# Three more groups of gate and up as seven block products, and the down weights' corner loads in two parts

## The reference

```
def swiglu(x, w_gate, w_up, w_down):          # 1024 x 2816, 1024 x 2816, 2816 x 1024
    return (jax.nn.silu(x @ w_gate) * (x @ w_up)) @ w_down

def half_ffn(h, l, j):
    y = swiglu(rms_norm(h, ffn_norm_pre[l, j]), ffn_w_gate[l, j], ffn_w_up[l, j], ffn_w_down[l, j])
    return h + 0.5 * rms_norm(y, ffn_norm_post[l, j])

for l in range(2):
    h = half_ffn(h, l, 0)
    h = h + rms_norm(mixer_l(rms_norm(h, ...)), ...)
    h = h + rms_norm(cross_attention(rms_norm(h, ...), mem, ...), ...)
    h = half_ffn(h, l, 1)
```

## Time and profile before

| | us |
|---|---|
| three timed executions | 2294.86, 2297.34, 2299.69 |
| their median | 2297.34 |
| the profiled execution's own time | 2292.94 |
| its span, first to last instruction | 2291.0 |
| PE busy | 2263.8 |
| DVE busy | 1483.9 |
| ACT busy | 1049.7 |
| mean granted clock of PE | 0.998 |

### The profile page before, as it was taken

The page is one execution under the profiler, slowest core; times in us unless marked ns, Lnnn a source line. Parts: engine busy times, 40 slices in busy tenths (PEclk is TensorE's granted clock), DMA queues, the critical chain, the costliest instruction groups (busy, mean ns, idle before and its releaser), DMA issues. The chain is left out here.

```text
span 2291.0 us, 32607 instructions
## 1 busy us (share of the span) xinstructions
PE 2263.8 (99%) x12963; PEld 1969.5 (86%) x12963; DVE 1483.9 (65%) x1913; ACT 1049.7 (46%) x1627; POOL 102.8 (4%) x145
## 2 busy tenths in 40 slices
PE   8999999999999999999999999999999999999998
PEld 7888888888888888889988889988878888888997
DVE  5757445586545658577757567746896565756774
ACT  5433324544544444435544435535265554343652
POOL 0000003100000000000010000000000000000000
PEclk9999999999999999999999999999999999999999
DMA  4342332321222233415534315542322222431563
GB/s 170 104 136 74 98 106 73 111 67 62 74 75 99 64 127 134 142 52 139 165 129 166 124 42 147 166 157 92 101 75 83 93 65 95 154 125 56 133 175 110
DMA packets 181757, 249.84 MB, mean 109 GB/s; under 512 B 13832, under 2 KB 125800, under 8 KB 181608
## 3 DMA queue, kind: packets, MB, share of 16 engines
q1 hardware_dynamic: 177176, 232.00, 31.2%
q0 software_dynamic: 4320, 15.73, 3.5%
q10 hardware_dynamic: 112, 0.03, 0.0%
HBM read 222.54 MB, written 9.44 MB: 101 GB/s over the span
## 5 line engine op out<-in xcount | busy, mean ns | idle before, releaser
L2477 PE MATMUL ps<-xlo,whi 128*128 128x512 f32 (+1 forms) x1936 | 670.9, 347 | 6.2 <-issue 4.1
L2479 PE MATMUL ps<-xhi,whi 128*128 128x512 f32 (+1 forms) x1936 | 668.1, 345 | 0.0
L2478 PE MATMUL ps<-xhi,wlo 128*128 128x512 f32 (+1 forms) x1696 | 600.4, 354 | 0.0
L1533 DVE TENSOR_TENSOR wlo<-raw,whi 128x1024 fp32r<-128x1024 f32 x251 | 306.3, 1223 | 323.0 <-ACT whi L917 320.6
L917 ACT ACTIVATE whi<-raw 128x1024 fp32r<-128x1024 f32 x281 | 294.9, 1054 | 340.8 <-PE ps L2479 298.4
L2477 PEld LDWEIGHTS ps<-xlo,whi 128*128 128x128 f32 x1936 | 367.4, 190 | 51.7 <-issue 7.5
L2479 PEld LDWEIGHTS ps<-xhi,whi 128*128 128x128 f32 x1936 | 367.3, 190 | 44.2
L2478 PEld LDWEIGHTS ps<-xhi,wlo 128*128 128x128 f32 x1696 | 321.4, 189 | 43.4
L1539 DVE SCALAR_TENSOR_TENSOR wlo<-raw,vec,whi 128x512 fp32r<-128x512 f32 (+1 forms) x224 | 154.8, 736 | 154.1 <-ACT whi L921 153.5
L921 ACT ACTIVATE whi<-raw,vec 128x512 fp32r<-128x512 f32 (+1 forms) x224 | 145.4, 702 | 197.9 <-PE ps L2479 163.2
L2477 PE MATMUL ps<-wlo,xhi 128*128 128x512 f32 x352 | 138.6, 394 | 1.1 <-issue 1.1
(11 more groups left out here) (322 smaller groups left out, 3829.4 us busy)
## 6 DMA issues: line engine op xcount, KB each, us to landing
raw<-ffn_w_gate_dram SPq DMA_DIRECT2D x176, 256.0 KB, 3.0
raw<-ffn_w_up_dram SPq DMA_DIRECT2D x176, 256.0 KB, 3.2
raw<-ffn_w_down_dram SPq DMA_DIRECT2D x96, 256.0 KB, 3.0
w<-ffn_w_down_dram SPq DMA_DIRECT2D x72, 256.0 KB, 5.4
raw<-xattn_w_kv_dram SPq DMA_DIRECT2D x64, 256.0 KB, 3.0
lo_aside<-raw POOLq DMA_DIRECT2D x30, 512.0 KB, 5.5
raw<-even_w_in_dram SPq DMA_DIRECT2D x56, 256.0 KB, 2.8
raw<-odd_w_in_dram SPq DMA_DIRECT2D x42, 256.0 KB, 2.9
```

The costliest lines, as they stand in the source:

```text
L1533: v.tensor_tensor(flat(wlo[:, slot]), flat(raw[:, from_slot]), flat(whi[:, slot]).bitcast(f32), SUB).then_inc(lo_made, 1)
L2477: mm(out_ap, lh, rl, start=start, stop=False, skip_group_check=skip_group_check)
L2478: mm(out_ap, ll, rh, start=False, stop=False, skip_group_check=skip_group_check)
L2479: return mm(out_ap, lh, rh, start=False, stop=stop, skip_group_check=skip_group_check)
```

## The change

`WOVEN` now holds groups 3, 4 and 5 too, so in the last three SwiGLUs the middle gate-and-up stage also runs as three woven groups: nine groups in all. `weave` on DVE takes the pass of the `quads` behind it and places the four corner combinations inside the stage's last group. The corner loads of that stage are issued in two parts, five behind group 3's weight loads and four behind group 4's, each part behind a wait of SP for the group's accumulation into the low part of B21.

```diff
-WOVEN = (6, 7, 8, 9, 10)
+WOVEN = (3, 4, 5, 6, 7, 8, 9, 10)
+ORDER_OF_CORNERS = [(corner, q) for corner in range(3) for q in range(QUADS)]
...
-                        if piece and after in pass_of and g == (2 if n == 0 else 1) and kp < 3:
-                            load_corners(pass_of[after], l, j, (kp,))
+                        if piece and after in pass_of and not scaled_rows(kind, l, arg) and g == (2 if n == 0 else 1) and kp < 3:
+                            load_corners(pass_of[after], l, j, [(kp, q) for q in range(QUADS)])
+                        if after in pass_of and scaled_rows(kind, l, arg):
+                            if n == 0 and g == 2 and kp < 3:
+                                load_corners(pass_of[after], l, j, [(kp, q) for q in range(QUADS)])
+                            if n == 1 and g < 2 and kp == 3:
+                                sp.wait_ge(raw_added[1], 16 * (woven_group[n_stage, g] + 1))
+                                first = ORDER_OF_CORNERS[:5] if g == 0 else ORDER_OF_CORNERS[5:]
+                                load_corners(pass_of[after], l, j, first)
...
-        def weave(w, group, mids, held_mid):
+        def weave(w, group, mids, held_mid, next_pass):
...
                     block_low(g, held)
+            if next_pass is not None:
+                t1_sums(next_pass)
             split_next()
...
             v.tensor_tensor(c11[:], y_out, c11[:], ADD).then_inc(c11_ready, 1)
             split_next()
+            if next_pass is not None:
+                t2_sums(next_pass, 0, late)
             dve.wait_ge(product_kept, 3 * w + 2)
             unit_done("T3")
             v.tensor_tensor(c22[:], x_out, c22[:], ADD).then_inc(c22_ready, 1)
             split_next()
+            if next_pass is not None:
+                t3_sums(next_pass, 0, late)
...
             split_next()
+            if next_pass is not None:
+                t4_sums(next_pass, 0, late)
             dve.wait_ge(gate_silu, mids).then_inc(bank_free[bank // 4], 1)
...
+                        if g == ng - 1 and not plain:
+                            split_next()
```

More of the change, by code:

```diff
@@ L618, in load, with load_corners @@
                 sp.dma_start(dst, src).then_inc(raw_full[slot], 16)
-        def load_corners(k, l, j, corners=range(3)):
+        def load_corners(k, l, j, corners=ORDER_OF_CORNERS):
             base, _, q0 = passes[k]
@@ L629, in load_corners @@
                     sp.wait_ge(pieces_used, base - 4 * FF_GROUPS[0][1] + 1 + SPLIT_SLOTS)
-            for n in corners:
+            for n, q in corners:
                 t, loaded, odd, c0 = ((w11, w11_loaded, 1, 0), (w12, w12_loaded, 1, GC), (w21, w21_loaded, 0, 0))[n]
-                for q in range(QUADS):
-                    k0 = (2 * (q0 + q) + odd) * P
-                    sp.dma_start(t[:, q, :], w[k0:k0 + P, c0:c0 + GC]).then_inc(loaded, 16)
+                k0 = (2 * (q0 + q) + odd) * P
+                sp.dma_start(t[:, q, :], w[k0:k0 + P, c0:c0 + GC]).then_inc(loaded, 16)
         def last_corner(w, k0, n):
@@ L2081, in _ @@
                         mids += 1
-                        weave(woven_group[n_stage, g], E.group, mids, held_mid)
+                        weave(woven_group[n_stage, g], E.group, mids, held_mid, pass_of.get(after) if g == ng - 1 else None)
                     for kp in range(0 if woven(kind, l, arg, g) else 4):
```

## The result

| | before | after |
|---|---|---|
| median of five timed executions, us | 2297.34 | 2304.82 |
| lowest and highest | 2294.84 to 2299.69 | 2303.43 to 2309.32 |
| ratio after to before, 95% interval | | 1.0034 [1.0023, 1.0045] |
| span of the profiled execution | 2291.0 | 2301.7 |

The prediction was 2294.7 us, with a range of 2286.5 to 2304.0: it missed by 10.1 us, and the sign was wrong.

What follows compares the result with a forecast made beforehand. PE bounds the kernel, with a DVE, ACT and DMA chain level with it in woven groups. Per stage 3.16 - 0.3 - 0.8 - 1.2 = 0.86 us gained, 2.6 in three stages: 2294.7 us, range 2286.5 to 2304.

Steps and rivals of the forecast that it cites:

- cover: In `quads` DVE is busy 26.1 of 28.7 us; the 2.6 us left was counted as enough for the combinations behind c22.
- (e): T4 of group 5 waits for DVE's add into c22, 3.1 us late, less 1.9 for PE's late start: 1.2 us.
- (a): Middle stage: seven products for eight take each group from 21.76 to 20.16 us, a ceiling of 4.80 us per stage.
- (b): Waits woven groups bring to the middle stage, taken from the last stage's first three groups: 1.64 us per stage.
- (d): DVE's block work (2.65 us) in groups 4 and 5 delays group 5's accumulation: 0 to 2.35 us, taken as 0.8.
- (c): Corner loads: SP's wait for group 3's B21 accumulation delays group 4's weights; 0 to 3.8 us per stage, taken as 0.3.
- The clock: The granted clock is at 1.00 of its 2.4 GHz level in every window read, so it was given no effect.
- the chain through DVE, ACT and the accumulation: Rival: this chain becomes the bound in the middle stage, 3.1 us lost per stage, 2306.6 us, slower; chance 0.15.
- the marks that I named for being wrong: Signs against: groups 4 and 5 start over 2 us late each, T4 of group 5 waits 3 us, or `quads` lengthens.

Runs made afterwards that it cites:

- e11: The changed kernel with only group 3 of the middle stage woven and the corner loads where the kernel before has them: 2293.40 us, ratio 0.9981.
- e5: The changed kernel with DVE's four block sums and first subtraction cut to one column where a woven group follows: 2296.57 us, ratio 0.9996.
- e3: The changed kernel with DVE's add into c22 moved ahead of the next split, T1 sum and second combination in every woven group: 2308.72 us, ratio 1.0050.
- e1: The changed kernel with each corner load of the middle stages moving one row of 128, SP's wait kept: 2303.03 us, ratio 1.0022.
- e6: The changed kernel with DVE's four corner combinations inside group 5 cut to one column: 2297.81 us, ratio 1.0003.
- e9: The changed kernel with DVE's two block subtractions moved behind the add into c22 in groups 4 and 5: 2308.02 us, ratio 1.0049.
- e4: The changed kernel with group 5 of the middle stage computed plainly again, corner loads unchanged: 2294.50 us, ratio 0.9990.
- e7: As e4, but no corner loads behind group 3: six behind group 4, three in group 5: 2291.81 us, ratio 0.9975.
- e8: The changed kernel run once more, unaltered, for its spread: 2306.33 us, ratio 1.0038.

## Why the prediction was wrong

**The step that failed.** Per stage the sum set 3.94 us of waits against a ceiling of 4.80 and kept 0.86. Measured in the first profile were 5.98 us of waits, and middle stage and `quads` together got 1.58 longer. Two places were put at nothing and cost 2.26 of it. T4 of groups 3 and 4 is not in the sum at all; it waited 1.49, as DVE's add into c22 comes behind a sum of late weights. `quads` was said to have cover enough; it grew by 0.77, as DVE's work did not fit. Term (e) was 0.4 too small, and the starts of groups 4 and 5 were 0.7 too large; 0.4 of the stage lies in gaps too short to list.

**What bounds the kernel, and (a).** Right. Where nothing waits a woven group takes 20.16 us in the middle stage too; e11 shows the 1.58 us of one group whole.

**(b) to (d), the starts of groups 4 and 5.** The sum was 2.74 us a stage; measured were 2.08 and 1.76 (0.31 + 1.77, 0.35 + 1.41). The size was near, the working was not. An accumulation that starts later by x was to land later by x, less something. The runs show that its landing hangs on the weight loads beside it. So (d)'s way, through ACT's negate, is refuted by e5: without the block work the accumulation for group 5 starts 15.35 us after group 4's start in the mean, with it 15.60, while the T4 sum and the loads behind it moved by 1.0.

**(c), corner loads: the step that looked at one consequence only.** SP's first corner load came at 948.20, 5.97 us after the group's start (about +6 was expected), and the weights behind it were late. I followed that to group 4's B11 alone, and put the price at 0.3. The T1 sum, which also needs those weights, stands ahead of the add into c22 on DVE, and so T4 of groups 3 and 4 waits: 0.87 + 0.62 and 0.67 + 0.73 us a stage, which no term of the sum had: (b) came from last-stage rows, in which T4 never waits. The wait at group 4's start was 0.31, as priced, but behind a T4 of group 3 that had waited already; e3, where it does not, has 1.34 there. e1 shows the cause for group 3 (0.87 to 0 without the data). The second part of the loads, which I had put at nothing, is among it (T4 of group 4, 0.62 to 0.11).

**(d), 0.8 us, mis-sized.** Cutting just its 2.65 us of work, in each of groups 4 and 5, shortened the middle stage by 3.1 us (66.10 to 62.98). The term was priced at the start of group 5 alone; the same lateness runs on to T4 of group 5 and, through the T4 sums, into the loads.

**(e), 1.2 us.** The place and the rule were right, the size was 1.64 and 1.91. Its second half failed: "2.6 us of cover, which I count as enough". `quads` grew by 0.77 us in each SwiGLU of the first profile, near the 1 us that I named as its price if the cover was gone, and e6 shows that the combinations do it. The work behind c22 is more than the cover, and DVE reaches the middle of `quads` late.

**The clock.** The prediction said that none of this is the clock's. That held in the SwiGLUs of the first profile. In the second, three stretches at the 1.2 GHz level came with the waits that the change brings.

**The rivals.** The one I gave 0.15, the chain through DVE, ACT and the accumulation, came near in size (2306.6 against 2304.8 and 2306.3) and in its point for it: 22.6 us of DVE work in group 5 against PE's 20.16. Its parts were not the ones listed, as a third of the waits was at T4 of groups 3 and 4 and in `quads`. I discounted it because "3.8 us of this stands behind c22 and may end in `quads`"; it did end there, and there was no room. Of the marks that I named for being wrong, `quads` getting longer is the one that showed.

## What to carry to other kernels

When a change makes the bounding engine cheaper and gives its work to another, add up that engine's work over the stage and the one behind it, and not only what stands ahead of the next wait: moving instructions (e3, e9) only moved the wait, and taking a group out of the plan (e4, e7, e11) gave the time back. For a load that comes late, list every instruction that waits for it and what is queued behind each on its engine. And try a change in parts: one of the three groups brought 1.58 us a stage, two with the loads later brought 2.02, all three lost 0.8 to 2.0 in the middle stage alone, and 1.2 of the 2.0 go with the lower clock and not with longer waits.

## What the hardware showed that I had not expected

An accumulating DMA that starts earlier need not land earlier. For group 4's B11 it was issued 15.4 to 16.3 us after group 3's start in the two profiles of the changed kernel, took 5.0 to 6.1 us and landed at +20.5 to +22.0. In e1 and e7, with the weights on time, it was issued at +13.1 to +13.3, took 6.7 to 8.4 and landed at +19.8 to +21.5. Some 2.6 us of earlier start gave 0.7 us in the mean. In both, group 4's weight loads are still landing while it runs; that sharing the DMA engines with them is what takes the gain is likely, and was not tested by itself.

The granted clock can fall to its 1.2 GHz level in the middle of a kernel whose PE is busy for 98% of the span: stretches of 3.4 to 6.8 us, 10 in the middle stages and 5 in the last stages of 42 SwiGLUs, each during or up to 1.5 us after a wait of PE of 1.9 to 3.4 us. It is read from windows over single stages and not from the mean, which was 0.994 in e8 and 0.997 in the first profile.
